# Routed experts by rounded halves, with blocks gathered and scattered by lists

## The reference, cut to what matters

```python
def moe_ffn(h, w_router, router_bias, w_e_gate, w_e_up, w_e_down, w_sh_gate, w_sh_up, w_sh_down):
    scores = sigmoid(h @ w_router)                       # (512, 64)
    ...  # the best 4 of 8 groups of experts, then the best 8 experts: top_e, weights wts
    # assignments sorted by expert, each expert padded to blocks of 128 rows:
    ...  # buf_tok (token of each row), buf_w (its weight), block_e (expert of each block)
    def expert_block(args):
        tok_b, w_b, e = args
        xb = h[tok_b]                                    # (128, 1024)
        hid = silu(xb @ w_e_gate[e]) * (xb @ w_e_up[e])  # (128, 256)
        return (hid @ w_e_down[e]) * w_b[:, None]
    out = lax.map(expert_block, (buf_tok.reshape(n_blocks, 128), buf_w..., block_e))
    routed = segment_sum(out.reshape(n_pad, d), buf_tok, num_segments=n_tok)
    shared = (silu(h @ w_sh_gate) * (h @ w_sh_up)) @ w_sh_down
    return routed + shared
```

## Time and profile before

| | us |
|---|---|
| median of 3 runs | 4518.5 |
| lowest and highest | 4512.3, 4520.8 |
| the profiled execution | 4512.0 |
| its span in the trace | 4509.8 |

### The profile page before, as it was taken

One profiled execution on the slowest core, in us unless ns is written; L12 is line 12 of the kernel. 1 busy time (PEld: TensorE's weight loads), 2 busy tenths in 40 slices (PEclk: granted clock), 3 DMA queues, 4 the chain that ended last, 5 costly groups with the idle time before them and its releaser, 6 DMA issues.

```text
span 4509.8 us, 41993 instructions
## 1 busy us (share of the span) xinstructions
PE 3844.8 (85%) x17200; PEld 2711.3 (60%) x17200; DVE 1173.0 (26%) x1770; ACT 1141.1 (25%) x1533; POOL 1051.2 (23%) x379
## 2 busy tenths in 40 slices
PE   4989895678955999999728999999879979876999
PEld 2875694447732444444326776776658848665887
DVE  3136424522151111111241222232321121223111
ACT  3225431123220111111023333333232222032221
POOL 0420123413421000000213222221134423123443
PEclk7999996788977999999859999999989989578999
DMA  4239215412218999999721111111022212011221
GB/s 158 74 132 421 92 65 224 187 75 75 94 65 329 338 342 343 344 343 338 304 91 60 47 51 43 47 47 57 28 84 94 99 42 75 0 38 65 100 96 66
DMA packets 102320, 628.46 MB, mean 139 GB/s; under 512 B 9154, under 2 KB 9426, under 8 KB 59924
## 3 DMA queue, kind: packets, MB, share of 16 engines
q1 hardware_dynamic: 67252, 486.39, 30.1%
q0 software_dynamic: 34912, 139.82, 7.6%
HBM read 469.93 MB, written 156.24 MB: 139 GB/s over the span
## 4 chain that ended last, share of the span: by engine, by line
PE 42%; DVE 3%; ACT 2%; POOL 2%; issue 1%; PEld 0%; DMA 0%; POOLq 0%; ACTq 0%; PEldq 0%; DVEq 0%
PE ps L261 9%; PE ps L262 9%; PE ps L263 9%; PE ps L1755 2%; PE ps L1730 2%; PE ps L1734 1%; PE ps L1703 1%; PE ps L1743 1%; PE ps L1715 1%; PE ps L1704 1%; PE ps L1705 1%; PE ps L2220 1%; PE ps L1719 1%; PE ps L2207 1%; POOL arena L1562 1%
## 5 line engine op out<-in xcount | busy, mean ns | idle before, releaser
L261 PE MATMUL ps<-arena_r,arena_r 128*128 128x512 f32 x2016 | 836.2, 415 | 107.7 <-POOL arena_r L252 38.7
L262 PE MATMUL ps<-arena_r,arena_r 128*128 128x512 f32 x2016 | 796.3, 395 | 0.0
L252 POOL TENSOR_TENSOR ring_r<-ring,arena_r 128x2048 fp32r<-128x2048 f32 x96 | 443.8, 4624 | 937.5 <-ACT arena_r L248 937.5
L261 PEld LDWEIGHTS ps<-arena_r,arena_r 128*128 128x128 f32 x2016 | 385.3, 191 | 223.5 <-issue 133.5
L248 ACT ACTIVATE arena_r<-ring 128x2048 fp32r<-128x2048 f32 x162 | 309.2, 1912 | 620.7 <-PE ps L263 457.0
L1501 PE MATMUL ps<-arena 128*128 128x512 f32 x1056 | 458.7, 592 | 0.0
L262 PEld LDWEIGHTS ps<-arena_r,arena_r 128*128 128x128 f32 x2016 | 385.6, 191 | 93.4 <-issue 18.3
L252 POOL TENSOR_TENSOR arena_r<-ring,arena_r 128x2048 fp32r<-128x2048 f32 x66 | 303.3, 4597 | 481.6 <-ACT arena_r L248 481.6
L263 PE MATMUL ps<-arena_r,arena_r 128*128 128x512 f32 x1056 | 411.9, 390 | 0.0
L263 PE MATMUL ps<-arena_r,ring_r 128*128 128x512 f32 x960 | 383.5, 400 | 0.0
L1501 PEld LDWEIGHTS ps<-arena 128*128 128x128 f32 x1056 | 198.1, 190 | 236.8 <-issue 236.8
(11 more groups left out here) (341 smaller groups left out, 5496.3 us busy)
## 6 DMA issues: line engine op xcount, KB each, us to landing
ring<-wstream SPq DMA_DIRECT2D x193, 1024.0 KB, 4.9
arena<-we_gu SPq DMA_DIRECT2D x66, 2048.0 KB
arena<-we_down SPq DMA_DIRECT2D x66, 1024.0 KB
xs<-rope POOLq DMA_DIRECT2D x12, 4096.0 KB, 20.1
ys<-rope POOLq DMA_DIRECT2D x12, 4096.0 KB, 13.6
arena<-xs SPq DMA_DIRECT2D x66, 512.0 KB, 9.4
ys<-arena SPq DMA_DIRECT2D x66, 512.0 KB, 8.6
arena<-x_t SPq DMA_DIRECT2D x1, 2048.0 KB, 8.8
```

The lines of the kernel that those rows point to most:

```text
L252: pool.tensor_tensor(whalf(c, 1), ring[:, c % NSLOT, :], whalf(c, 0).bitcast(F32), ALU.subtract).then_inc(sem("chunk_lo"), 1)
L261: pe.matmul(out, hi, rhs[0], start=start, stop=False)
L262: pe.matmul(out, hi, rhs[1], start=False, stop=False)
```

## The change

The products of the experts go by rounded halves. In each pair of blocks ScalarE rounds three pieces of 128x2048 per block (gate-up in two pieces, down in one), VectorE makes the low halves of the gate-up pieces in place, GpSimd those of down; the turned inputs and hidden rows are split by ScalarE and VectorE. Each product becomes three matmuls. TensorE's order in a pair interleaves the two blocks and turns the inputs of the pair after while it multiplies; the last pair stands behind the loop without that. On ScalarE and VectorE the work for the next pair's weights stands among that of this pair. Block rows are no longer stored in an array of padded rows: the 512 token rows are stored once (`h2`), GpSimd gathers each block's 128 rows by a list of indices (`IDX_X`) and scatters each block's results to the place that belongs to the assignment (`IDX_Y`); indices out of range stand for padding and are skipped. The lists come from 32 products of one-hot rows that VectorE makes (64 instructions). The two fills are gone. The combination loads 32 contiguous pieces of 512 KB by SyncE, and TensorE turns each group of 128 tokens once its 8 are summed.

```diff
-        def fill_gpsimd(pool):
-            for i in range(MAXBLK // NFILL):
-                pool.wait_ge(sem("da_exp"), 4 * i + 1)
-                fill(pool, xs, i)
...
+        def gather_x(pool, col, s):
+
+            pool.tensor_copy(COLS[s], IDX_X[:, col]).then_inc(sem("moe_x_col"), 1)
+            pool.wait_ge(sem("moe_x_col"), 1)
+            pool.sem_inc(sem("moe_x_col"), -1)
+            pool.indirect_dma_start(XB[s], None, h2, bass.IndirectOffsetOnAxis(ap=COLS[s], axis=0), bounds_check=T - 1,
+                                    oob_is_err=False).then_inc(sem(f"moe_x{s}"), 16)
...
+            pe.wait_ge(sem("rt_experts"), 1)
+            pe.wait_ge(sem("h2_tok"), 8)
+            pe.matmul(bank(5, MAXBLK)[0:1], BECOL, C["ident"][:, 0:MAXBLK], start=True, stop=True).then_inc(sem("rt_turned"), 1)
+
             chunk_done(shared(0, 1))
+
+            for n in range(32):
+                pe.wait_ge(sem("rt_hot"), n + 1)
+                mm = pe.matmul(bank(2, NCOL), HOT_SLOT[:, n, :], HOT_BLOCK[:, n, :], start=(n == 0), stop=(n == 31))
+            mm.then_inc(sem("rt_listed"), 1)
...
+            for n in range(32):
+                dve.tensor_scalar(HOT_SLOT[:, n, :], IOTA, SLOT[:, n:n + 1], None, ALU.is_equal)
+                dve.tensor_scalar(HOT_BLOCK[:, n, :], BLOCK_AT, BASE[:, n:n + 1], ROW1[:, n:n + 1], ALU.is_equal,
+                                  ALU.mult).then_inc(sem("rt_hot"), 1)
...
+            dve.wait_ge(sem("rt_listed"), 1)
+            row = bank(2, NCOL)
+            link(dve.tensor_scalar(NO_ROW, row, 0.0, SPARE, ALU.is_equal, ALU.mult))
+            link(dve.scalar_tensor_tensor(IDX_Y, row, -1.0, NO_ROW, ALU.add, ALU.add))
+            dve.tensor_scalar(IDX_X, IDX_Y, FAR + T - 1, None, ALU.bitwise_and).then_inc(sem("rt_rows"), 1)
...
+                    for j in range(2):
+                        sp.wait_ge(sem("moe_gu_used"), i * 4 + (2 * s + j + 1))
+                        sp.dma_start(arena[:, EW[s][j]:EW[s][j] + CHW],
+                                     we_gu[bass.ds(e * 2 + j, 1)].rearrange("o p n -> (o p) n")).then_inc(sem(f"moe_w{s}{j}"), 16)
...
+            for n in range(32):
+                t, k = divmod(n, 8)
+                if n >= 8:
+                    sp.wait_ge(sem("g_used"), n - 7)
+                sp.dma_start(GB[n % 8], ys[k * T + t * P:k * T + t * P + P, :]).then_inc(sem(f"gathered{n % 8}"), 16)
...
+            def pair_of_blocks(i, back):
+                gate_up(i, 0, back)
+                if not back:
+                    pe.wait_ge(sem("moe_x0"), i * 16 + 32)
+                    pe.wait_ge(sem("moe_y0"), i + 1)
+                    turn(0)
+                gate_up(i, 1, back, "moe_x_free0" if not back else None)
+                turn_hidden(i, 0, back)
+                if not back:
+                    pe.wait_ge(sem("moe_x1"), i * 16 + 32)
+                    pe.wait_ge(sem("moe_y1"), i + 1)
+                    turn(1)
+                down_ready(i, 0, back)
+                down(0, 0, "moe_x_free1" if not back else None)
+                turn_hidden(i, 1, back)
+                down(0, 1).then_inc(sem("moe_d_used"), 1)
+                down_ready(i, 1, back)
+                down(1, 0)
+                down(1, 1).then_inc(sem("moe_d_used"), 1)
...
+        def moe_scalar(act):
...
+            def pair_of_blocks(i, back):
                 for s in range(2):
...
+                    high(s, 2, i * 16 + (16 - 16 * back))
+                silu(i, 0, back)
+                if not back:
+                    turned(0, i + 2)
+                    high(0, 0, i * 16 + 32)
+                silu(i, 1, back)
+                hidden(i, 0, back)
+                if not back:
+                    turned(1, i + 2)
+                hidden(i, 1, back)
+                if not back:
+                    high(0, 1, i * 16 + 32)
+                act.wait_ge(sem("moe_d_used"), i * 2 + (3 - 2 * back))
+                act.wait_ge(sem("moe_out0"), i * 16 + (16 - 16 * back))
+                act.activation(YO[0], pf[:, 0:1024], ACT.Copy).then_inc(sem("moe_y0"), 1)
+                act.activation(small[:, 60:61], epst[:, :], ACT.Copy).then_inc(sem("moe_y_full0"), 1)
+                if not back:
+                    for j in range(2):
+                        high(1, j, i * 16 + 32)
...
+        def moe_vector(dve):
+            def low(s, j, highs):
+                dve.wait_ge(sem("moe_gu_hi"), highs)
+                dve.tensor_tensor(expert_lo(s, j), expert_raw(s, j), expert_hi(s, j).bitcast(F32),
+                                  ALU.subtract).then_inc(sem("moe_gu_lo"), 1)
...
+        def moe_gpsimd(pool):
+            def pair_of_blocks(i, more):
                 for s in range(2):
...
+                    pool.wait_ge(sem("moe_d_hi"), 1)
+                    pool.sem_inc(sem("moe_d_hi"), -1)
+                    pool.tensor_tensor(expert_lo(s, 2), expert_raw(s, 2), expert_hi(s, 2).bitcast(F32),
+                                       ALU.subtract).then_inc(sem("moe_d_lo"), 1)
+                if more:
+                    for s in range(2):
+                        next_x(i * 2 + (s + 4), s)
                 for s in range(2):
...
+                    pool.wait_ge(sem(f"moe_y_full{s}"), 1)
+                    pool.sem_inc(sem(f"moe_y_full{s}"), -1)
+                    pool.tensor_copy(COLS[2 + s], IDX_Y[:, bass.ds(i * 2 + s, 1)]).then_inc(sem("moe_y_col"), 1)
+                    pool.wait_ge(sem("moe_y_col"), 1)
+                    pool.sem_inc(sem("moe_y_col"), -1)
+                    pool.indirect_dma_start(ys, bass.IndirectOffsetOnAxis(ap=COLS[2 + s], axis=0), YO[s], None,
+                                            bounds_check=8 * T, oob_is_err=False).then_inc(sem(f"moe_out{s}"), 16)
...
-            pe.wait_ge(sem("g_used"), 32)
-            for j in range(KT):
-                for t in range(TT):
+            for t in range(TT):
+                pe.wait_ge(sem("g_used"), 8 * t + 8)
+                for j in range(KT):
                     mm = pe.matmul(bank(j, P, t * P), H2TOK[:, t, j * P:j * P + P], C["ident"], start=False,
                                    stop=(t == TT - 1), skip_group_check=True)
```

More of the change, by code:

```diff
@@ L1295, in rt_tensor, with rt_gpsimd @@
+        def rt_gpsimd(pool):
+            pool.dma_start(view(T0, 324), iota_t).then_inc(sem("iota_loaded"), 16)
+            for s in range(2):
+                pool.dma_start(view(SINK + 64 * s, 64)[0:1, :], iota_t[0:1, 0:64]).then_inc(sem(f"moe_out{s}"), 16)
+            pool.wait_ge(sem("h2_stored"), 16)
+            pool.wait_ge(sem("rt_rows"), 1)
+            for s in range(2):
+                gather_x(pool, slice(s, s + 1), s)
         def rt_tensor(pe):
@@ new lines, in moe_sync @@
+            sp.wait_ge(sem("h2_tok"), 8)
+            sp.dma_start(h2.rearrange("(t p) d -> p t d", p=P), H2TOK).then_inc(sem("h2_stored"), 16)
+            sp.wait_ge(sem("rt_blocks"), 1)
+            first = [sp.value_load(BEI[0:1, s:s + 1], min_val=0, max_val=E_N - 1) for s in range(2)]
+            for s in range(2):
+                load_gate_up(s, first[s])
+            for s in range(2):
+                load_down(s, first[s])
+            sp.wait_ge(sem("stage_ended"), 4 * MOE_STAGE)
+            n = pairs(sp)
@@ new lines, in moe_vector, with turned, value, hidden @@
+        def moe_vector(dve):
[3 more added lines that the diff above has]
+                                  ALU.subtract).then_inc(sem("moe_gu_lo"), 1)
+            def turned(s, n):
+                dve.wait_ge(sem(f"moe_xt_hi{s}"), n)
+                dve.tensor_tensor(XBT[s][1], pf[:, 1024 * s:1024 * s + 1024], XBT[s][0].bitcast(F32),
+                                  ALU.subtract).then_inc(sem(f"moe_xt{s}"), 1)
+            def value(i, s, back):
+                dve.wait_ge(sem(f"moe_silu{s}"), i + (1 - back))
+                dve.tensor_tensor(HID[s], SIL[s], bank(4 + s, 256, 256), ALU.mult).then_inc(sem(f"moe_hid{s}"), 1)
+            def hidden(i, s, back):
+                dve.wait_ge(sem(f"moe_hidt_hi{s}"), i + (1 - back))
+                dve.tensor_tensor(HIDT[s][1], bank(6 + s, 256), HIDT[s][0].bitcast(F32),
+                                  ALU.subtract).then_inc(sem(f"moe_hidt{s}"), 1)
+            def pair_of_blocks(i, back):
+                value(i, 0, back)
+                if not back:
+                    turned(0, i + 2)
+                    low(0, 0, i * 4 + 5)
+                value(i, 1, back)
+                hidden(i, 0, back)
+                if not back:
+                    turned(1, i + 2)
+                hidden(i, 1, back)
+                if not back:
+                    low(0, 1, i * 4 + 6)
+                    low(1, 0, i * 4 + 7)
+                dve.wait_ge(sem("moe_d_used"), i * 2 + (4 - 2 * back))
+                dve.wait_ge(sem("moe_out1"), i * 16 + (16 - 16 * back))
+                dve.tensor_copy(YO[1], pf[:, 1024:2048]).then_inc(sem("moe_y1"), 1)
```

(13 more changed lines are left out.)

329 lines of the change are left out of this document (176 added, 153 removed).

## The result

| | before | after |
|---|---|---|
| median, us | 4516.4 (4 runs, 4512.3 to 4520.8) | 4582.1 (4 runs, 4579.3 to 4583.0) |
| ratio | | 1.0144, 95% interval 1.0127 to 1.0162 |
| profiled execution, us | 4512.0 | 4583.0 |

The account below looks back on a forecast made before the run. TensorE was taken to bound the kernel before, DMA close behind. Routing 57, loop start 8, pairs 744, tail 7 and combination 52 make 868 against 985.7 us, 118 less: 4512 - 118 = 4394 us, range 4320 to 4465.

Parts of the forecast that it names:

- What bounds the kernel before: Expert loop before the change: TensorE bounds it, DMA close behind; a pair of blocks takes 24.54 us.
- TensorE by halves: Expert products: three matmuls at 0.2267 us replace 0.86 us; TensorE needs 18.8 us per pair, 5.7 less.
- Exclusion of weight subtractions: VectorE's four and GpSimd's two weight subtractions per pair exclude each other: 4 x 2.3 + 2 x 4.6 = 18.4 us.
- The ring: Expert loop: chain of releases through VectorE, TensorE, ScalarE and GpSimd that closes after one pair, sum 22.6 us.
- The bounds: Limits for one pair in the expert loop: 19.4 us at least, 25.4 us at most.
- The clock: Expert loop: a clock under 1 was left out because TensorE stays 83% busy; listed as a sign of being wrong.
- the 3 to 4 forecast: Expert loop: TensorE waits 3 to 4 us per pair, before the second gate-up half or before down.
- the fourth rival: Loop's indirect DMAs cost 7.4 us each with freshly written index columns: GpSimd 38.8 us per pair, 4929 us; chance 0.06.
- break-even: Expert loop: at 3.95 us per indirect DMA GpSimd's pair is 26.2 us, eating the 54 us saved elsewhere.
- DMA and the weights: Loop loads: 7.3 MB per pair if out-of-range rows are skipped, 17.9 to 21.4 us, under 22.6; reloads outside the chain.
- Routing 57, combination 52, fills 0: Stages around the loop: routing 57 us instead of 96, combination 52 instead of 69.4, removing the fills gains 0.

Follow-up runs that it names:

- f32 kernel with a better order: Changed kernel with all halves of the experts undone (plain f32 products), lists, interleaved order and combination kept: 4407.2 us, ratio 0.9751 to the kernel before.
- one tiny subtraction: Changed kernel with only the second of GpSimd's two down-weight subctractions (s1) cut to 64 columns: 4434.9 us, ratio 0.9806 to the kernel before.

## Why the prediction was wrong

- **What bounds the kernel before**: right. The f32 kernel with a better order gave 22.76 us, TensorE at 500 of 500 us.
- **TensorE by halves**: right. Steps of 0.227 us in after where the clock is full (0.2267).
- **Exclusion of weight subtractions**: right that they exclude each other, and a low half of 2.29 us as counted (2.3); who goes first was not asked.
- **The ring, its last term, is the step that failed**: "GpSimd low half of down weights 4.6; then VectorE's first low half may go". It may not: it waits for the second as well, in 28 of 32 pairs. The run with one tiny subtraction prices it: 4.61 us per pair, 33 x 4.61 = 152 us of the 188 between forecast and result. The bounds did not save it: the upper one, 25.4, had VectorE behind the second subtraction by 0.5 us, not by all of it. The rest of the ring came out. In the pair shown, from the end of that low half (1723.11) to GpSimd's next subtraction (1740.06), it takes 16.95 us, where its terms add up to 15.7.
- **The clock, left out because TensorE would stay 83% busy**: the second error, and the 1.25 us just named. TensorE was busy for 73% and the granted clock 0.86. Its six down matmuls of the ring took 1724.01 to 1726.73, 2.72 us, where the ring has 1.36 + 0.08: 1.3 us per pair. With one tiny subtraction, where the wait is 3.3 us, within the 3 to 4 forecast, the same six still took 2.55 us (1736.35 to 1738.90), 1.1 us more than counted, and its ordinary pair is 1.1 us over the 22.6. 22.6 + 4.6 + 1.1 = 28.3, beside 28.4 measured for ordinary pairs. That the clock alone makes these 1.1 us was not isolated by a run.
- **GpSimd's indirect DMAs**: the fourth rival, the one that ended slower, was not the cause: median 1.04 and 1.00 us, none at 7 in the loop. Only 0.88 us of idling ahead of each, put down to a register step, and the copies and indirect DMAs that wait for VectorE's low halves (longest 2.28 and 3.15 us), were missed; none of that decides in after. But its arithmetic held: it put break-even at 26.2 us per pair, and 33 x (28.04 - 26.2) = 61 us stands beside the 66 measured. That arithmetic came out for a cause that was not the one named. The sign was wrong since no mechanism but that one was followed beyond 25.4 us.
- **DMA and the weights**: right that the ring doesn't pass them: ScalarE waits 34.5 and 13.5 us in 700 for weights, but GpSimd's first subtraction (1711.87) follows its own scatter (ends 1711.84) at once. Rows out of range do cost no transfer: GpSimd's queue moved 33.6 MB from 1347 to 2298 us, 4096 rows of 4 KB gathered and as many scattered, not 8448 each.
- **Routing 57, combination 52, fills 0**: right: 58.1, 53.0, and nothing that a run shows. In routing a one-hot row took 0.22 us (64 of them, 1331.98 to 1345.95), where I had taken 0.18.

The chances gave 0.06 to slower, by one rare mechanism. A ring whose longest term depends on which of two queued instructions is served first deserved a rival of its own: had VectorE been placed behind both subtractions, 27.2 us per pair, the sum would have been 4394 + 33 x 4.6 = 4546 before any loss of clock.

## What to carry to other kernels

Where VectorE and GpSimd exclude each other, the sum of their exclusive work can matter less than what stands behind a blocked instruction. Keep subtractions with two SBUF inputs away from the evacuations that TensorE waits for (5.0 us per pair here), and count whole GpSimd subtractions that stand back to back as one block. When a step at TensorE waits several us in each round, price the time at half clock behind it as well (1.1 to 1.3 us here). A subtraction of 128x2048 took 2.3 us on VectorE and 4.6 on GpSimd: moving it to VectorE, which had room, gave another 2.2 us per pair.

## What the runs showed of the hardware

- A low half of VectorE that is issued in the first of two back-to-back GpSimd subtractions of 128x2048 waits for both (28 of 28, up to 9.98 us for 2.29 of work). If the second has 64 columns (22 of 22), or a 128x1 copy follows (31 of 31), VectorE goes ahead of it.
- It goes the other way as well: GpSimd's copy of a 128x1 column, 0.2 us, took 2.28 us behind a VectorE subtraction, and an indirect DMA, 1.0 us, took 2.78:

```profile
1732.42 2.29 DVE L1661 TENSOR_TENSOR arena_r<-arena,arena_r 128x2048 fp32r<-128x2048 f32 x1 [0.51 <-ACT arena_r L1612]
1732.84 2.78 POOL L1725 DMA_INDIRECT ys<-arena  x1 [0.88 <-POOLq L1724]
```

- An indirect DMA whose rows are half out of range lands after 4.1 us (gather, median), and moves only the rows in range. The HBM bytes written fall from 156 to 41 MB, of which the 24 fills of 4 MB are 101; the 32 loads of 512 KB in the combination ran at 392 GB/s.
